# Latent attention: rope queries with their high and low halves in one tile, a bank freed by ScalarE, five output tiles together

## What is computed

```python
c_q = rms_norm(z[..., :o1], q_norm_g)
c_kv = rms_norm(z[..., o1:o2], kv_norm_g)
k_rope = rope(z[..., o2:o3][:, :, None, :], pos)[:, :, 0, :]
q = (c_q @ w_uq).reshape(B, S, MLA_HEADS, MLA_NOPE + MLA_ROPE)
q_rope = rope(q[..., MLA_NOPE:], pos)
...
s = jnp.einsum('bqhc,bkc->bhqk', qb, k_cat)   # q_cat = [nope part, rope part], one rope key for all heads
s = jnp.where(key_idx[None, :] <= q_idx[:, None], s, neg)
pr = jax.nn.softmax(s, axis=-1)
...
return (jax.nn.silu(gate) * o) @ w_out
```

## Time and profile before

| | |
|---|---|
| median of three runs | 2301.42 us (2300.96 to 2301.71) |
| the profiled execution, its own time | 2301.16 us |
| its span in the profile | 2299.2 us |
| TensorE busy | 2198.7 us, 96% of the span |
| VectorE busy | 1185.5 us, 52% |
| ScalarE busy | 861.3 us, 37% |
| GpSimd busy | 968.7 us, 42% |

### The profile page before, as it was taken

One profiled execution on the slowest core, in us unless ns is written; L12 is line 12 of the kernel. 1 busy time (PEld: TensorE's weight loads), 2 busy tenths in 40 slices (PEclk: granted clock), 3 DMA queues, 4 the chain that ended last, 5 costly groups with the idle time before them and its releaser, 6 DMA issues.

```text
span 2299.2 us, 29536 instructions
## 1 busy us (share of the span) xinstructions
PE 2198.7 (96%) x10336; PEld 1820.5 (79%) x10336; DVE 1185.5 (52%) x1714; ACT 861.3 (37%) x1264; POOL 968.7 (42%) x706
## 2 busy tenths in 40 slices
PE   6999999999999999988999999999999989999997
PEld 4888888677788888866888888887788777888885
DVE  5756546876666666667265222225455446222224
ACT  4423233454444444444444223224424434323223
POOL 4253535354433333324445445444423223455443
PEclk8999999999999999999999999999999989999998
DMA  4322222232222222222322222223211111222321
GB/s 147 92 97 74 97 83 85 84 128 93 74 73 73 76 85 77 78 78 90 112 74 92 105 96 91 94 107 110 91 56 63 67 55 44 103 91 91 109 92 55
DMA packets 37838, 200.03 MB, mean 87 GB/s; under 512 B 4331, under 2 KB 9707, under 8 KB 15372
## 3 DMA queue, kind: packets, MB, share of 16 engines
q1 hardware_dynamic: 28496, 188.76, 23.2%
q10 hardware_dynamic: 9276, 10.37, 1.4%
HBM read 193.87 MB, written 5.24 MB: 87 GB/s over the span
## 4 chain that ended last, share of the span: by engine, by line
PE 85%; DVE 9%; ACT 2%; DVEq 2%; issue 1%; DMA 0%; SPq 0%; ACTq 0%
PE bank L415 16%; PE bank L416 15%; PE bank L419 15%; PE bank L402 12%; PE bank L403 12%; PE bank L404 12%; ACT WH L991 1%; DVE PKL L1552 1%; DVE X L1770 1%; DVE T L1768 1%; DVE SS L1571 1%; DVE R L1560 1%; DVE T L1697 1%; DVE HL L1566 1%; DVE MYL L1552 0%
## 5 line engine op out<-in xcount | busy, mean ns | idle before, releaser
L354 POOL TENSOR_TENSOR WL<-RAW,WH 128x512 fp32r<-128x512 f32 x700 | 965.0, 1410 | 1301.6 <-ACT WH L991 1301.6
L991 ACT ACTIVATE WH<-RAW 128x2048 fp32r<-128x2048 f32 (+1 forms) x181 | 335.9, 1856 | 643.9 <-PE bank L404 321.5
L415 PE MATMUL bank<-HH,WH 128*128 128x512 f32 x968 | 389.2, 402 | 9.2 <-DVEq L2209 5.9
L416 PE MATMUL bank<-HL,WH 128*128 128x512 f32 x968 | 381.4, 394 | 0.0
L419 PE MATMUL bank<-HH,WL 128*128 128x512 f32 x968 | 239.2, 389 | 0.0
L415 PEld LDWEIGHTS bank<-HH,WH 128*128 128x128 f32 x968 | 184.4, 191 | 51.8 <-DVEq L2209 6.4
L416 PEld LDWEIGHTS bank<-HL,WH 128*128 128x128 f32 x968 | 184.4, 190 | 39.7 <-issue 2.2
L419 PEld LDWEIGHTS bank<-HH,WL 128*128 128x128 f32 x968 | 181.7, 188 | 37.8
L2056 DVE TENSOR_TENSOR X<-X,bank 128x512 f32<-128x512 f32 x128 | 87.6, 687 | 196.7 <-PE bank L419 117.4
L402 PE MATMUL bank<-HH,WH 128*128 128x512 f32 x352 | 138.4, 393 | 17.6 <-POOL WL L354 11.7
L2047 DVE SCALAR_TENSOR_TENSOR TG<-bank,RS 128x512 f32<-128x512 f32 x64 | 44.0, 688 | 205.1 <-PE bank L404 135.8
(11 more groups left out here) (410 smaller groups left out, 4464.9 us busy)
## 6 DMA issues: line engine op xcount, KB each, us to landing
RAW<-panels SPq DMA_DIRECT2D x175, 1024.0 KB, 4.8
X<-xin SPq DMA_DIRECT2D x4, 512.0 KB, 9.2
xsave<-X ACTq DMA_DIRECT2D x4, 512.0 KB, 2.8
X<-xsave ACTq DMA_DIRECT2D x1, 2048.0 KB, 8.3
TAB<-scratch ACTq DMA_DIRECT2D x16, 128.0 KB, 2.8
out<-ACC SPq DMA_DIRECT2D x8, 256.0 KB, 2.5
RS<-decay ACTq DMA_DIRECT2D x4, 256.0 KB, 2.4
scratch<-O SPq DMA_DIRECT2D x4, 256.0 KB
```

The source lines that it names most:

```text
L354: gp.tensor_tensor(WL[:, s, cs], RAW[:, s, cs], WH[:, s, cs].bitcast(f32), ALU.subtract).then_inc(lo_ready, 1)
L415: nc.tensor.matmul(o, wh[:, columns[k - k0]], xh[:, k, :], start=first and k == k0, stop=False)
L416: nc.tensor.matmul(o, wh[:, columns[k - k0]], xl[:, k, :], start=False, stop=False)
L991: return nc.scalar.activation(dst, src, ACT.Copy)
```

## The change

It does four things, all in the latent attention.

1. **`QR` in place of `QRH` and `QRL`.** `QR` has one slot per head. In head a's slot its own 64 rows hold the high half of the rope query, and the other 64 rows hold the low half of the same head. Since the rope key stands in both halves of the rows, one matmul over 128 rows, `QR` by `KRH`, gives high by high and low by high together. A second matmul over the 64 own rows, `QR[own]` by `KRL[own]`, gives high by low. The rope part of a score tile is two matmuls, 128 and 64 rows deep, where it was three of 128.
2. **Splits.** `KRH` and `KRL` are unmasked and made by one instruction each. The query's split becomes two instructions of 64 rows each on ScalarE and two on VectorE, the latter writing the other half of the rows.
3. **The bank behind `straight`** is freed by ScalarE, which drains right behind the copy, and no longer by VectorE in `turned`.
4. **Output tiles:** five instead of four go together; the fifth is the one in bank 1.

```diff
-            KRH, KRL = sb("KRH", [128, 2, 512], f32r, c), sb("KRL", [128, 2, 512], f32r, c)
+            KRH, KRL = sb("KRH", [128, 512], f32r, c), sb("KRL", [128, 512], f32r, c)
...
-            QRH, QRL = sb("QRH", [128, 512], f32r, c), sb("QRL", [128, 512], f32r, c)
+            QR = sb("QR", [128, 2, 512], f32r, c)
...
+        own = [slice(64 * a, 64 * a + 64) for a in range(2)]
...
-                    mm3(o, QRH[:, qs], QRL[:, qs], KRH[:, a, 0:m], KRL[:, a, 0:m], False, True)\
+                    nc.tensor.matmul(o, QR[:, a, qs], KRH[:, 0:m], start=False, stop=False)
+                    nc.tensor.matmul(o, QR[own[a], a, qs], KRL[own[a], 0:m], start=False, stop=True)\
                         .then_inc(S["mla_s_made"], 1)
...
-                ends = tiles_together([bank(4 + f) for f in range(4)], w, 1024, MYH, MYL, 2,
+                ends = tiles_together([bank(b) for b in (4, 5, 6, 7, 1)], w, 1024, MYH, MYL, 2,
...
-                    end = ends[f] if f < 4 else tile_of(bank((1, 3, 0, 2)[f - 4])[:, :], w, f, 1024, MYH, MYL, 0, 2)
+                    end = ends[f] if f < 5 else tile_of(bank((3, 0, 2)[f - 5])[:, :], w, f, 1024, MYH, MYL, 0, 2)
...
+            def high_rope():
+                for a in range(2):
+                    hi(QR[own[a], a, :], TG[own[a], 0, :]).then_inc(S["mla_rope_hi"], 1)
...
-            def straight(src, dst):
-                nc.scalar.activation(dst, src, ACT.Copy).then_inc(S["mla_straight"], 1)
+            def straight(b, dst):
+                nc.scalar.activation(dst, B[b][:, :], ACT.Copy).then_inc(S["mla_straight"], 1)
+                act.drain().then_inc(free[b], 1)
...
-                v.tensor_tensor(straight, straight, COS2[:, :], ALU.mult).then_inc(free[b_straight], 1)
+                v.tensor_tensor(straight, straight, COS2[:, :], ALU.mult)
...
-                ve.wait_ge(S["mla_rope_hi"], n * 1 + 3)
-                lo(QRL[:, :], TG[:, 0, :], QRH[:, :]).then_inc(S["mla_rope_split"], 1)
+                for a in range(2):
+                    ve.wait_ge(S["mla_rope_hi"], n * 2 + (a + 2))
+                    end = lo(QR[own[1 - a], a, :], TG[own[a], 0, :], QR[own[a], a, :])
+                end.then_inc(S["mla_rope_split"], 1)
```

More of the change, by code:

```diff
@@ L166, in program @@
         FREQ1 = CONST[:, 384:385]
-        OF_HEAD = [CONST[:, 386 + a:387 + a] for a in range(2)]
         TO_NEAR, TO_FAR = CONST[:, 416:544], CONST[:, 544:672]
@@ L1264, in _ @@
             act.wait_ge(panel_used, N_MLA)
-            straight(B[0][:, :], T[:, 2, :])
+            straight(0, T[:, 2, :])
             root("ckv", KV_LORA)
@@ L1270, in _ @@
             act.wait_ge(S["mla_rope_f32"], 1)
-            for a in range(2):
-                nc.scalar.activation(KRH[:, a, :], T[:, 2, :], ACT.Copy, scale=OF_HEAD[a]).then_inc(S["mla_rope_hi"], 1)
+            hi(KRH[:, :], T[:, 2, :]).then_inc(S["mla_rope_hi"], 1)
             high_qk(0, "q1", 3, MADE_FIRST)
             act.wait_ge(S["mla_qk_made"], MADE_FIRST["rope"])
-            straight(B[0][:, :], TG[:, 0, :])
+            straight(0, TG[:, 0, :])
             high_qk(0, "k0", 1, MADE_FIRST)
@@ L1279, in _ @@
             act.wait_ge(S["mla_rope_f32"], 2)
-            hi(QRH[:, :], TG[:, 0, :]).then_inc(S["mla_rope_hi"], 1)
+            high_rope()
             high_values(0, (0, 1), N_MLA + 2)
@@ L1328, in pair @@
                     act.wait_ge(S["mla_qk_made"], n * 4 + 8)
-                    straight(B[3][:, :], TG[:, 0, :])
+                    straight(3, TG[:, 0, :])
                 high_probabilities(1)
@@ L1816, in _, with turned @@
             scaled("latent", KC, ACC[:, KQ:KQ + KC, :], ("kvn", 0), CKH, CKL, "latent_split", KQ)
-            def turned(copy, straight, temp, b_straight, b_swapped):
+            def turned(copy, straight, temp, b_swapped):
                 ve.wait_ge(S["mla_swapped"], copy)
                 v.tensor_tensor(temp, B[b_swapped][:, :], SIN2[:, :], ALU.mult).then_inc(free[b_swapped], 1)
-                v.tensor_tensor(straight, straight, COS2[:, :], ALU.mult).then_inc(free[b_straight], 1)
+                v.tensor_tensor(straight, straight, COS2[:, :], ALU.mult)
                 ve.drain()
@@ L1846, in _ @@
             ve.wait_ge(S["sines"], 4)
-            turned(1, T[:, 2, :], T[:, 3, :], 0, 1)
+            turned(1, T[:, 2, :], T[:, 3, :], 1)
             ve.drain()
@@ L1850, in _ @@
             low_qk(0, "q0", 2, FIRST)
-            ve.wait_ge(S["mla_rope_hi"], 2)
-            for a in range(2):
-                end = v.scalar_tensor_tensor(KRL[:, a, :], T[:, 2, :], OF_HEAD[a], KRH[:, a, :].bitcast(f32),
-                                             ALU.mult, ALU.subtract)
-            end.then_inc(S["mla_rope_split"], 1)
+            ve.wait_ge(S["mla_rope_hi"], 1)
+            lo(KRL[:, :], T[:, 2, :], KRH[:, :]).then_inc(S["mla_rope_split"], 1)
             low_qk(0, "q1", 3, FIRST)
@@ L1858, in _ @@
             low_qk(0, "k1", 2, FIRST)
-            turned(2, TG[:, 0, :], TG[:, 1, :], 0, 3).then_inc(S["mla_rope_f32"], 1)
+            turned(2, TG[:, 0, :], TG[:, 1, :], 3).then_inc(S["mla_rope_f32"], 1)
             v.memset(ACC[:, :, :], 0.0)
@@ L1936, in pair @@
                 if not last:
-                    turned(n * 1 + 3, TG[:, 0, :], TG[:, 1, :], 3, 1).then_inc(S["mla_rope_f32"], 1)
+                    turned(n * 1 + 3, TG[:, 0, :], TG[:, 1, :], 1).then_inc(S["mla_rope_f32"], 1)
                     low_rope(n + 1)
@@ L2295, in _constants @@
     c[:, 384] = (10000.0 ** (-p / 128.0)).astype(np.float32)
-    c[:, 386] = p < 64
-    c[:, 387] = p >= 64
     moves = np.zeros((2, 128, 128), np.float32)
```

## The result

The changed kernel takes 2312.96 us, the median of five runs (2312.42 to 2321.67). The kernel before ran beside it: five runs of 2300.96 to 2301.71. The ratio of after to before is 1.006, with a 95% interval of 1.0043 to 1.0078: slower by 0.6%. The prediction had 2313 us and 2305 to 2321.

What follows compares the result with a forecast made beforehand. TensorE's own work, the spacing of its matmuls, was taken as the bound. Calls +11.5, first call +1.2, prologue -1.3, tails +0.3 and last tiles +0.4 summed to +12.1 us: 2313 us, range 2305 to 2321.

Steps and rivals of the forecast that it cites:

- Part 1: In the latent attention's scores, one matmul of six fewer per tile saves TensorE 0.635 us a call.
- part 2: In the scores, eight depth switches around the 64-row matmuls cost 0.15 to 0.20 us each, 1.45 us a call.
- The first call: First scores call, at half the clock: switches cost 2.4 us, the removed product saves 1.2, net +1.2 us.
- Part 3, the prologue: Before the first scores, `rope_tile`'s bank wait goes (-2.0 us) and an extra VectorE split adds 0.7: -1.3 us.
- Part 3, the tail: At a looped pair's end, the removed bank wait is lost in a longer wait for `MYL`, late by 0.7 us.
- The rival of the late tail: Splits, drain and `MYL` delay output tiles' k = 1 by 1.7 us, seven pairs add 7 us: 2320 us; chance 0.10.
- Part 4: Five output tiles together put three more products ahead of the `MYL` wait, ending a pair 0.68 us earlier from `MYL`.
- The last pair: First scores call grows 0.82 us, the second's growth vanishes in a 2.35 us wait, later output tiles add 0.4.

Runs made afterwards that it cites:

- experiment 1: Changed kernel with the last product of a score tile over all 128 rows, adding low by low: 2291.01 us, ratio 0.9945 to the kernel before.
- experiment 5: Changed kernel with the 64-row matmul first in every second score tile, so two are neighbours and switches halve: 2308.76 us, ratio 1.0025 to the kernel before.
- experiment 2: Kernel before with only the bank behind `straight` freed by ScalarE with its drain, and five output tiles together: 2300.92 us, ratio 0.9986.
- experiment 4: Changed kernel with the bank behind `straight` freed by VectorE again, without ScalarE's drain: 2319.28 us, ratio 1.0078 to the kernel before.
- experiment 7: Changed kernel, 64-row products kept, with second head's gating and its split ahead of rope and panel splits: 2305.16 us, ratio 1.0013 to the kernel before.
- experiment 3: Changed kernel with four output tiles together instead of five: 2323.62 us, ratio 1.0087 to the kernel before.
- experiment 6: Kernel of experiment 1 with second head's gating and its split moved ahead of rope and panel splits: 2283.66 us, ratio 0.9915 to the kernel before.
- experiment 8: Kernel of experiment 6 with four output tiles together instead of five: 2278.34 us, ratio 0.9896 to the kernel before.

## Why the prediction was right, and where it was only lucky

The two profiled executions differ by 11.1 us of span (2310.3 less 2299.2). Place by place:

| place | predicted, us | measured, us |
|---|---|---|
| up to the first scores | -1.3 | -0.9 (prologue -1.3, ahead of it +0.4) |
| pair 0 | +2.1 | +4.5 |
| pairs 1 to 6 | 6 x 1.69 = +10.1 | 6 x 1.98 = +11.9 |
| last pair | +1.2 | +0.75 |
| rest of the program | 0 | -5.1 |

- **Part 1 and part 2, the calls.** Predicted +0.82 us a call, measured 4.54 - 3.81 = 0.73 and 0.11 behind the call: 0.84. Experiments 1 and 5 show the cause, and both put a switch at 0.19 us, within the 0.15 to 0.20 that was read from the earlier trace rows. The lone matmul's loss spreads over the two starts behind it, which is why the call alone looks cheaper than it is. The weight loads of the changed profile, late at both changes of depth, bear out the reading behind the term. The Trainium skill, page "TensorEngine Tiling (Array Packing)", section "Key Properties", has a drain of TensorE at a change of tiling mode. The runs agree: 0.19 us a change here. The Trainium skill, page "TensorE: Matmul & The Clock Gate", section "Why this matters for your kernels", has a single small-K matmul at the time of a full one. That holds here for its duration (0.27 us at 128 columns and either depth); what a lone one costs its neighbours stands beside that.
- **The first call.** Predicted +1.2, measured 8.02 - 6.71 = +1.31. What was missed is behind it. TensorE's granted clock went to half at 581.3 us before and 579.7 after, and came back at 588.1 and 593.3: 6.83 against 13.65 us. The call ends at 589.13 us after the change, and from there to 593.3 ten 512-column matmuls start 0.43 us apart in place of 0.23, some +2.1 us. With the second call's 0.85 and the tail's 0.27 (below) this makes the +4.5 of pair 0.
- **Part 3, the prologue.** Right: the 1.9 us wait is gone. From the first matmul on `CQH` to the first scores it is 28.11 us before and 26.77 after, -1.34. By experiment 2 the release alone gives -1.90 (26.21 us), by experiment 4 the second split alone +0.85 (28.96). The first scores start only 0.9 us earlier because the profiled run of the changed kernel reached that first matmul 0.4 us later (554.34 against 553.91 us). That is clock: from the first matmul on `GH` of the layer before, at 451 us, it is 103.5 to 103.6 us in the three profiles with a stretch at half clock at 467 us (after, experiments 1 and 7) and 102.2 in the seven without.
- **Part 3, the tail.** The step was right (the wait moves to `MYL`, and the bank's gain is lost in it), and its terms were too small. One split was put at 0.54 us and is 0.77; the drain was put at 0.1 and is 0.2. `MYL` is 0.95 us late and not 0.7. TensorE's wait was put at 1.3 and is 1.46. The rival of the late tail asked for 1.7 us; its premise, a `MYL` of 1.45 us, is the same before and after, and so adds nothing.
- **Part 4.** Predicted -0.68 a pair; experiment 3 has -0.69. So a tail is +0.95 - 0.68 = +0.27 and not +0.05, 1.5 us more in the loop. Of the 4 us by which the sum was too low (below), these tails are 1.5 and the longer half clock behind the first call is 2.1.
- **The last pair.** +0.82 and +0.4 predicted, +0.75 measured. The steps hold. The first transpose behind the second call comes 25.19 us behind the pair's start before and 26.02 after, +0.83, the first call's growth, and the wait of the earlier trace rows falls from 2.35 us to 0.06: it did take up the second call's growth. The five tiles cost 0.36 by experiment 2 against before, and 0.74 by experiments 6 and 8, each with 0.6 us more of half clock in the kernel with five. What makes up for them fits the clock, though no run isolates it: behind that transpose the changed kernel has 7.2 us at half clock where the one before has 10.2.
- **The rest of the program.** Put at nothing. It is 5.1 us shorter in the profiled run with the same 5718 matmuls. No step of the change reaches there, and the table above has the same three levels for every kernel: the run of before fell in the middle one and that of after in the lowest. This hides the errors above. At the start of the next layer the changed kernel is 16.2 us behind, where the sum had 12.1: it was about 4 us too low, and still in its range. The 2313 was luck by that much.

What stays open: why the half clock at the first scores lasts twice as long. In all five profiles of kernels with the 64-row product (after, experiments 3, 4, 5, 7) it lasts 13.65 us, and in all five without (before, 1, 2, 6, 8) 6.83 us. The clock falls while TensorE waits for the rope split, and that wait grew from 3.4 to 6.6 us. But experiment 1 has the wait of 6.6 us too, and 6.83 us of half clock. So the product brings it, and with half the switches (experiment 5) it still does; by what was not tried.

## What to carry to other kernels

Before a matmul is made shallower than its neighbours, price its two switches from the trace (here 0.19 us each): a lone 64-row matmul costs nearly 0.4 us more than a full one, so fill the spare rows, or put shallow ones side by side. When a wait is removed, follow the engine to its next wait and see what ends that one; if the work that was added sits ahead of it, the gain is gone. And order what TensorE waits for next (the gating and its split) ahead of what is needed a whole stage later (the rope split, the weight panel): that was worth 1.74 us a pair, more than any one step of the change gains.

## What the runs showed of the hardware

- At one depth the weights of a matmul are loaded from the start of the matmul before it; at a change of depth, either way, they are loaded 0.33 to 0.43 us behind that start (512 columns). The loss lies partly behind the switch: in a row 512 columns wide the starts are 0.33, 0.43 and 0.34 us apart around one 64-row matmul, where 0.22 to 0.23 is normal.
- Two 64-row copies on ScalarE take 1.28 us where one of 128 rows takes 0.63, and two 64-row subtractions on VectorE 1.39 us where one takes 0.69: half the rows is not half the time. The second copy puts the next instruction back by 0.77 us: each of the two following starts is 0.65 to 0.66 us behind the one before it, where it is 0.54 behind the copy of 128 rows.
- The low half of `MYL` takes 1.43 us beside GpSimd's first `WL` instructions and 0.69 us ahead of them. In the trace of the kernel before, of 148 instructions of its form with no GpSimd work beside them and 49 with it that read a bank, none took over 0.70 us; of 85 with it and both inputs in SBUF, 43 took over 0.8.
- Ten runs of one kernel spread over 8 to 10 us by the granted clock (experiment 5: 2300.39 us at 0.985, 2310.05 us at 0.978). The same 5718 matmuls took 1256, 1261 or 1266 us, with 27 to 58 us at half clock. A step of 0.5 us in a pair can't be told from medians; it is plain in the trace.
